# Reading activations backwards, weights in pairs and rows at other offsets in a two-block transformer kernel

## What is computed

```python
h = x
h = h + _hybrid_mixer(_rmsnorm(h, ...), ..., w_out)                 # 4 kinds of recurrent / linear attention heads
h = h + _memory_cross_attn(_rmsnorm(h, ...), mem_n, wq, wk, wv, wo) # attention on 256 memory rows
h = h + _conv_ffn(_rmsnorm(h, ...), w_up, conv_w, w_down)           # "ffn", 2 x 2816 columns up
x = _rmsnorm(h, final_norm_w)
for l in range(2):                                                  # the second block, DEPTH_2 = 2
    x, ctx = both through ffn_half_step(...)                        # "a1" for l = 0, "b1" for l = 1
    mixer: fourier_sgu_mixer for l = 0 ("ab_*"), attention with rope for l = 1 ("k2", "q2", "v2", "wo2")
    x (and ctx where it lives on) through ffn_half_step(...)        # "a2" for l = 0, "b2" for l = 1
return rms_norm(x, g_final_2)
```

## Time and profile before

| | |
|---|---|
| time, median of 2 runs | 2109.5 us (2108.54 and 2110.46) |
| profiled execution, span from the first to the last instruction | 2103.2 us |
| median less span | 6.3 us |
| TensorE busy | 2039.4 us, 97% |
| VectorE, ScalarE, GpSimd busy | 1172.1, 821.9, 225.2 us |

### The profile page before, as it was taken

One profiled execution on the slowest core, in us unless ns is written; L12 is line 12 of the kernel. 1 busy time (PEld: TensorE's weight loads), 2 busy tenths in 40 slices (PEclk: granted clock), 3 DMA queues, 4 the chain that ended last, 5 costly groups with the idle time before them and its releaser, 6 DMA issues.

```text
span 2103.2 us, 30887 instructions
## 1 busy us (share of the span) xinstructions
PE 2039.4 (97%) x13254; PEld 1787.7 (85%) x13254; DVE 1172.1 (56%) x1579; ACT 821.9 (39%) x1051; POOL 225.2 (11%) x185
## 2 busy tenths in 40 slices
PE   7988999999999999999999999999999999999998
PEld 6985998999888888888888888888888888878998
DVE  6778555767643654453555442235766744755454
ACT  6742455655532222243342222234222223455444
POOL 1000000403111001100101001110100111001111
PEclk9999999999999999999999999999999999999999
DMA  6425654454642543352344332234545533304553
GB/s 243 161 82 181 221 200 181 162 189 156 220 176 75 195 159 119 123 182 81 123 158 154 123 136 88 82 128 162 193 158 199 199 126 114 126 21 161 178 181 113
DMA packets 54136, 317.05 MB, mean 151 GB/s; under 512 B 6000, under 2 KB 12400, under 8 KB 23792
## 3 DMA queue, kind: packets, MB, share of 16 engines
q1 hardware_dynamic: 50848, 308.99, 41.4%
q10 hardware_dynamic: 3152, 6.10, 0.9%
HBM read 314.01 MB, written 1.05 MB: 150 GB/s over the span
## 4 chain that ended last, share of the span: by engine, by line
PE 86%; DVE 6%; ACT 4%; issue 3%; DMA 0%; SPq 0%; POOL 0%; DVEq 0%; ACTq 0%; POOLq 0%
PE psum L279 27%; PE psum L281 26%; PE psum L280 26%; ACT w_hi L255 2%; PE psum L1736 1%; PE psum L1334 1%; DVE w_lo L263 1%; PE psum L1317 1%; DVE xc L1525 0%; PE psum L1345 0%; DMA raw<-in_w_in_r 0%; PE psum L932 0%; DVE normed_lo L1916 0%; PE psum L933 0%; DVE small L1399 0%
## 5 line engine op out<-in xcount | busy, mean ns | idle before, releaser
L279 PE MATMUL psum<-normed_hi,w_hi 128*128 128x256 f32 (+1 forms) x2600 | 859.0, 330 | 18.5 <-DVE normed_lo L475 8.4
L280 PE MATMUL psum<-normed_lo,w_hi 128*128 128x256 f32 (+1 forms) x2600 | 848.3, 326 | 0.0
L281 PE MATMUL psum<-normed_hi,w_lo 128*128 128x256 f32 (+1 forms) x2600 | 848.0, 326 | 0.0
L263 DVE TENSOR_TENSOR w_lo<-raw,w_hi 128x2048 fp32r<-128x2048 f32 (+1 forms) x246 | 510.7, 2077 | 389.6 <-ACT w_hi L255 388.8
L279 PEld LDWEIGHTS psum<-normed_hi,w_hi 128*128 128x128 f32 x2600 | 492.2, 189 | 70.8 <-issue 21.9
L280 PEld LDWEIGHTS psum<-normed_lo,w_hi 128*128 128x128 f32 x2600 | 492.5, 189 | 43.3 <-issue 1.2
L281 PEld LDWEIGHTS psum<-normed_hi,w_lo 128*128 128x128 f32 x2600 | 492.4, 189 | 42.1
L255 ACT ACTIVATE w_hi<-raw 128x2048 fp32r<-128x2048 f32 (+1 forms) x246 | 421.7, 1714 | 161.7 <-PE psum L281 157.3
L279 PE MATMUL psum<-h_hi,w_hi 128*128 128x512 f32 (+1 forms) x913 | 310.7, 340 | 2.0 <-POOL h_lo L1681 1.7
L281 PE MATMUL psum<-h_hi,w_lo 128*128 128x512 f32 (+1 forms) x913 | 309.6, 339 | 0.0
L280 PE MATMUL psum<-h_lo,w_hi 128*128 128x512 f32 (+1 forms) x913 | 309.3, 339 | 0.0
(11 more groups left out here) (383 smaller groups left out, 1364.3 us busy)
## 6 DMA issues: line engine op xcount, KB each, us to landing
raw<-in_mod SPq DMA_DIRECT2D x72, 1024.0 KB, 4.8
raw<-in_a_up SPq DMA_DIRECT2D x42, 1024.0 KB, 4.8
raw<-in_b_up SPq DMA_DIRECT2D x42, 1024.0 KB, 4.8
raw<-in_ffn_up SPq DMA_DIRECT2D x22, 1024.0 KB, 4.8
raw<-in_a_down SPq DMA_DIRECT2D x32, 704.0 KB, 4.1
raw<-in_b_down SPq DMA_DIRECT2D x32, 704.0 KB, 4.1
raw<-in_ffn_down SPq DMA_DIRECT2D x16, 704.0 KB, 4.1
raw<-in_wo SPq DMA_DIRECT2D x8, 1024.0 KB, 4.7
```

The source lines that it names most:

```text
L263: dve.tensor_tensor(w_lo[:, slot, 0:size], raw[:, raw_slot(("main", g)), 0:size], w_hi[:, slot, 0:size].bitcast(F32), ALU.subtract).then_i ...
L279: pe.matmul(out, lh, rh, start=first, stop=False, skip_group_check=group)
L280: pe.matmul(out, lh, rl, start=False, stop=False, skip_group_check=group)
L281: return pe.matmul(out, ll, rh, start=False, stop=last, skip_group_check=group)
```

## The change

Three things are altered, stage by stage, by two tables of names.

- "backward": the moving activations are read from the last column to the first (`columns_of` gives a slice with step -1), and the output in PSUM is written from the last column to the first too (`made`), so each result lands where it was.
- "pairs": the split weights of a chunk lie interleaved, hi and lo of one weight side by side. ScalarE and VectorE write them, and LDWEIGHTS reads them, with a step of 8 bytes where it was 4. `w_hi` and `w_lo` are now one tensor, `w_parts`; in the other stages hi and lo are its two halves.
- rows: the hidden activations begin at column 40 (first half) and 24 (second half) in `ffn` and at column 12 in `b2`, where it was 8; the activations of both `up` jobs of `b1` begin at column 16, where it was 0.

The number and the order of the instructions on every engine stay as they were, and so do their shapes.

```diff
+WEIGHT_ORDER = {
+    "w_out": "backward", "wk": "pairs", "wq": "backward pairs",
+    "ffn_up0": "backward", "ffn_up1": "backward pairs",
+    "a1_up0": "backward", "a1_up1": "pairs", "a1_down0": "backward pairs", "a1_down1": "backward",
+    "a2_up0": "backward pairs", "a2_down0": "pairs",
+    "b1_up1": "backward", "q2": "pairs", "b2_up0": "backward", "b2_up1": "backward pairs",
+}
+HIDDEN_SHIFT = {"ffn": (40, 24), "b2": (12, 12)}
...
-        w_hi = sb("w_hi", [P, SLOTS, CHUNK], F32R)
-        w_lo = sb("w_lo", [P, SLOTS, CHUNK], F32R)
+        w_parts = sb("w_parts", [P, SLOTS, 2 * CHUNK], F32R)
+        w_hi, w_lo = w_parts[:, :, 0:CHUNK], w_parts[:, :, CHUNK:2 * CHUNK]
+        w_pair = w_parts[:, :, :].rearrange("p s (c two) -> p s c two", two=2)
...
+        def split_out(g, low):
+
+            slot, size = g % SLOTS, sizes[g]
+            if "pairs" in WEIGHT_ORDER.get(job_at[g], ""):
+                return w_pair[:, slot, 0:size, low]
+            return w_parts[:, slot, low * CHUNK:low * CHUNK + size]
+
+        def tile_of(s, i):
+
+            order = WEIGHT_ORDER.get(s.job.name, "")
+            cut = slice(i * P, (i + 1) * P)
+            if "pairs" in order:
+                return w_pair[:, s.slot, cut, 0], w_pair[:, s.slot, cut, 1]
+            return w_hi[:, s.slot, cut], w_lo[:, s.slot, cut]
+
+        def columns_of(s, cut):
+
+            if "backward" in WEIGHT_ORDER.get(s.job.name, ""):
+                return slice(cut.stop - 1, cut.start - 1 if cut.start else None, -1)
+            return cut
+
+        def moved(s, a, k, span):
+            return a[:, k, columns_of(s, span)]
+
+        def made(s, n, span):
+            return psum[:, s.bank + n, columns_of(s, span)]
...
-            act.activation(w_hi[:, slot, 0:size], raw[:, raw_slot(("main", g)), 0:size], ACT.Copy).then_inc(hi_ready, 1)
+            act.activation(split_out(g, 0), raw[:, raw_slot(("main", g)), 0:size], ACT.Copy).then_inc(hi_ready, 1)
...
-            dve.tensor_tensor(w_lo[:, slot, 0:size], raw[:, raw_slot(("main", g)), 0:size], w_hi[:, slot, 0:size].bitcast(F32),
+            dve.tensor_tensor(split_out(g, 1), raw[:, raw_slot(("main", g)), 0:size], split_out(g, 0).bitcast(F32),
...
-                            w = slice((n * k_tiles + k) * P, (n * k_tiles + k + 1) * P)
-                            mm = three_passes(pe, psum[:, s.bank + n, 0:span.stop - span.start],
-                                              (w_hi[:, s.slot, w], w_lo[:, s.slot, w]),
-                                              (act_hi[:, k, span], act_lo[:, k, span]), k == k_order[0], k == k_order[-1])
+                            w = n * k_tiles + k
+                            mm = three_passes(pe, made(s, n, slice(0, span.stop - span.start)),
+                                              tile_of(s, w),
+                                              (moved(s, act_hi, k, span), moved(s, act_lo, k, span)), k == k_order[0], k == k_order[-1])
...
-                self.hidden = slice(0, w) if w > T else slice(SHIFT, SHIFT + w)
+                self.hidden = [slice(at, at + w) for at in HIDDEN_SHIFT.get(name, (0, 0))]
...
+                self.hi, self.lo = (a[:, at:at + KT * 2 * T].rearrange("p (k t) -> p k t", k=KT) for a in (normed_hi, normed_lo))
...
-        n23, n24 = modulated_halves(3, "a2_down1"), modulated_halves(4, "b1_down1")
+        n23, n24 = modulated_halves(3, "a2_down1", at_column=16), modulated_halves(4, "b1_down1")
```

More of the change, by code:

```diff
@@ L245, in load @@
             sp.dma_start(raw[:, at % SLOTS, 0:size], src).then_inc(raw_landed[at % SLOTS], 16)
+        job_at = [job.name for job in jobs.values() for c in range(job.n)]
+        def split_out(g, low):
[17 more added lines that the diff above has]
+            return psum[:, s.bank + n, columns_of(s, span)]
         def split_hi(act, g):
@@ L313, in pe_begin @@
                 for n in range(2):
-                    w = slice((n * KT + k) * P, (n * KT + k + 1) * P)
-                    three_passes(pe, psum[:, s.bank + n, 0:span.stop - span.start], (w_hi[:, s.slot, w], w_lo[:, s.slot, w]),
-                                 (act_hi[:, k, span], act_lo[:, k, span]), k == 0, False)
+                    w = n * KT + k
+                    three_passes(pe, made(s, n, slice(0, span.stop - span.start)), tile_of(s, w),
+                                 (moved(s, act_hi, k, span), moved(s, act_lo, k, span)), k == 0, False)
         def pe_token_major(pe, job, act_hi, act_lo, span, after_tile=None, after_k=None):
@@ L347, in pe_tile_by_tile @@
                 for k in k_order:
-                    w = slice((n * k_tiles + k) * P, (n * k_tiles + k + 1) * P)
-                    mm = three_passes(pe, psum[:, s.bank + n, 0:T], (w_hi[:, s.slot, w], w_lo[:, s.slot, w]),
-                                      (act_hi[:, k, X], act_lo[:, k, X]), k == k_order[0], k == k_order[-1])
+                    w = n * k_tiles + k
+                    mm = three_passes(pe, made(s, n, X), tile_of(s, w),
+                                      (moved(s, act_hi, k, X), moved(s, act_lo, k, X)), k == k_order[0], k == k_order[-1])
                 if n == 0:
@@ L1575, in pe @@
                         before_down()
-                    pe_feature_major(pe, down, h_hi, h_lo, self.hidden, n_tiles=1, k_tiles=HALF, before_k=hidden_k,
+                    pe_feature_major(pe, down, h_hi, h_lo, self.hidden[half], n_tiles=1, k_tiles=HALF, before_k=hidden_k,
                                      in_halves={KT - 1: closing.pe_last} if half and closing is not None else None)
@@ L1603, in evac @@
                         act.wait_ge(evacuated, s.g + 1)
-                        out = h_hi[r, s.c:s.c + 1, self.hidden]
+                        out = h_hi[r, s.c:s.c + 1, self.hidden[half]]
                         act.activation(out, b[r, 1:2, 0:self.w], ACT.Copy).then_inc(ff_hi, 1)
@@ L1829, in pe_last @@
                                 self.pe_sums(pe, 0)
-                            w = slice((n * k_tiles + k) * P, (n * k_tiles + k + 1) * P)
-                            mm = three_passes(pe, psum[:, s.bank + h, n * T:(n + 1) * T], (w_hi[:, s.slot, w], w_lo[:, s.slot, w]),
-                                              (act_hi[:, k, t], act_lo[:, k, t]), at == 0, at == k_tiles - 1)
+                            w = n * k_tiles + k
+                            mm = three_passes(pe, made(s, h, slice(n * T, (n + 1) * T)), tile_of(s, w),
+                                              (moved(s, act_hi, k, t), moved(s, act_lo, k, t)), at == 0, at == k_tiles - 1)
                     if h == 0:
@@ L1845, in pe_first @@
                         for n in range(n_tiles):
-                            w = slice((n * k_tiles + k) * P, (n * k_tiles + k + 1) * P)
-                            mm = three_passes(pe, psum[:, s.bank + n, t], (w_hi[:, s.slot, w], w_lo[:, s.slot, w]),
-                                              (act_hi[:, k, t], act_lo[:, k, t]), k == 0, k == k_tiles - 1)
+                            w = n * k_tiles + k
+                            mm = three_passes(pe, made(s, n, t), tile_of(s, w),
+                                              (moved(s, act_hi, k, t), moved(s, act_lo, k, t)), k == 0, k == k_tiles - 1)
                 return mm
@@ L1881, in act_high_half @@
                     act.wait_ge(n_scaled, self.scaled_base + h * KT + k + 1)
[L1882 removed]
+                    act.activation(self.hi[:, k, t], nrm[:, k, t], ACT.Identity, bias=self.shift(k, h)).then_inc(n_hi, 1)
             def act_rest(self, act):
```

19 lines of the change are left out of this document (9 added, 10 removed).

## The result

The changed kernel takes 2134.8 us (2134.77 and 2134.88) where the kernel before takes 2109.5 us: ratio 1.0119, interval 1.0101 to 1.0138, or + 25.3 us. That is inside the range and within 2%, but it isn't the forecast of no change: all of the interval lies above 1.

A forecast was written before the change was run, and what follows sets the result against it. TensorE, busy 97% of the 2103.2 us span, bounds the kernel through its matmul paces. Zero for backward and pairs, - 0.3 us for ffn_down1, and 6.3 us from span to median gave 2109 us; range 2088 to 2175, the case's own 2095 to 2117.

The forecast's parts named there:

- I take zero for both: In the sum over touched TensorE stages: neither reading direction nor load step changes the pace, so backward and pairs add nothing.
- an effect of the size seen between two layouts, 3.3 ns: Upper bound for backward's 4,689 matmuls: the pace difference between aligned rows and rows shifted by 32 bytes at 256 columns.
- the prediction's own sign of being wrong: TensorE's pace within chunks: the forecast is wrong if several large stages move by over 5 ns.
- Pairs at 256 shifted columns: 888 matmuls of pairs with shifted rows: forecast zero; touched shifted stages losing 3.3 ns would add 5.4 us over 1,608 matmuls.
- 48 bytes: Rows at 12 columns in b2_down: 528 matmuls, between 0 and + 3.3 ns each, at most + 1.8 us.
- `ffn_down1`: Rows again 32 bytes behind a multiple of 64: 264 matmuls 1.1 ns faster if they take wk's rhythm, - 0.3 us.
- 64 bytes in `b1_up0`: Rows at 16 columns, a multiple of 64 bytes: claimed to cost nothing.
- The rival of pairs: Weight loads cost their reads twice: + 40 us (2149) if overhead doubles, + 153 us (2262) if load time doubles; chance 0.18.
- The rival of backward: Backward is a slow stream on TensorE: 9.0 ns per matmul makes 42 us, 14 ns + 66, half rate + 737; chance 0.12.
- The rule on the loads' step: SBUF lines are 16 bytes and two hits hide the access, so weight loads at an 8-byte step cost nothing.
- The streams out of each other's way: The change removes the per-matmul overhead of 13.3 or 10.0 ns on TensorE: wholly 72 us, giving 2037 us; chance 0.11.
- The splits: VectorE's stepped splits slow down and bound ffn_up1 (+ 9 us) and q2 (+ 2): + 11 us, 2120 us; chance 0.06.

The follow-up runs named there:

- u_rows: Changed kernel with only the moved rows kept, weights in one tensor as two halves, nothing backward or in pairs: 2111.7 us, ratio 1.0009.
- d_sides: Changed kernel with single causes per stage: only the read or only the output backward, weights some columns later, or pairs; some stages combined: 2133.2 us.
- s_rows1: Changed kernel with rows and weights at many different offsets, one combination per stage, all read forward and contiguous: 2124.8 us.
- s_apart: Kernel before with empty space between hi and lo activations, normed_lo 64 bytes and h_lo 128 bytes further on: 2130.6 us.
- n_narrow: Changed kernel with another table: in eight stages each weight load brings 64 columns instead of 128, half the outputs left out: 2117.7 us.
- best1: Kernel before with ffn_up0 and ffn_up1 backward, k2 and q2 rows at column 8, and h_lo pushed 128 bytes away: 2112.2 us, ratio 1.0016.

## Why the prediction was wrong

**The step that failed** is "I take zero for both" in the sum, with the bound under it, "an effect of the size seen between two layouts, 3.3 ns". The 3.3 ns is the difference between two layouts at 256 columns. At 512 columns showed one layout only, so there was no row for the effect there, and I put the same bound on it. The effect there is twice as large, and a loss: 233.3 less 226.7 is 6.7 ns (both rounded), for backward, for pairs and for both. 2,727 matmuls of 512 columns x 6.7 = + 18.2 us, and + 17.8 in the times of these stages. That is the prediction's own sign of being wrong: several large stages moved by over 5 ns. What the rows did show, that the offset moves the overhead and that one layout has several rhythms, should have widened the case's own range (2095 to 2117), not left zero as its middle. That 2134.8 lies in the stated range all the same is luck: the range reached so far because of the rivals, and none of them happened as priced.

**The other terms.** Pairs at 256 shifted columns: 888 matmuls, + 3.3 ns, + 2.9 us, the bound that I had written beside it. Pairs at 256 aligned columns (`q2`): nothing, as forecast. Backward at 256 aligned columns (`ffn_up0`): - 1.5 ns, which would be - 0.8 us, but - 0.3 us in the stage, as the distances across every second chunk edge grew from 0.31 to 0.39 us. At shifted ones `w_out` and `b2_up0` rose by 1 ns, but both have 117.7 to 117.9 in u_rows with no edit, so that isn't shown to be the price of backward. 48 bytes: + 0.8 us between 0 and 1.8. `ffn_down1`: + 0.5 us instead of - 0.3. 64 bytes in `b1_up0`: + 1.0 us instead of nothing; I had only the multiple of 64 in mind, and the untouched kernel has nothing at 512 columns that isn't at column 0.

**The rival of pairs** was right that pairs costs something, wrong in size and in its reason. 13.3 ns at aligned rows were 6.7 at 512 columns and 0 at 256, so the overhead doesn't go with the stretch that a load covers; no load took twice its time, as no stage came near 213 ns at 256 columns.

**The rival of backward** put the price on a slow stream, 9 ns or more. The stream costs 6.7 ns at 512 columns, - 1.5 at 256 aligned ones, and at shifted ones nothing that can be told from the 1 ns of untouched stages. The rule of the Trainium skill that stood beside it (Advanced Engine Details and Errata, PSUM Cachelines) doesn't bite on a descending output: written backward alone, `a1_up1` kept 226.8 ns.

**The rule on the loads' step.** The Trainium skill (Advanced Engine Details and Errata, SBUF Cachelines) asks for at least two hits on a line to hide the access. I read it as no cost for a step of 8 bytes. But TensorE's pace rose by 6.7 ns in `a1_up1` with nothing but pairs, and ScalarE's copy into the 8-byte step by 0.28 us, VectorE's by nothing. So in this case the step wasn't free for TensorE at 512 columns and for ScalarE, though two elements share a line; but reading backward, with contiguous columns, costs the same 6.7 ns, so the step isn't shown to be the reason as such.

**The streams out of each other's way** came true in `ffn_up0` alone, by 1.5 ns of 13.3. **The splits** I charged with 11 us or nothing; 1.2 us show in `ffn_up1`, by ScalarE's copy, which I had not looked at, and not by VectorE's.

**Two readings of the prediction** were off, and the forecast didn't rest on them: its 2,217 matmuls "of 512" columns hold 258 that run on 256, in the chunks made by halves, and from the earlier trace rows the room beside a load at 256 columns is 17 to 20 ns (117 to 120 less 100), not 10.

In the list of what would show it I named `b1_up1` for backward and `b1_up0` for 64 bytes; both did, at 233.3 and 228.8, though `b1_up1` has the 64 bytes as well. With backward alone (u_backward) it has 233.3 too.

**What stays open** is what the streams share. Shown: the cost of backward is in reading the moving operand, and the place of the load alone costs as well (d_sides); what counts of the places is each offset and not their difference alone (s_rows1), and the distance of the two moving tensors (s_apart); in `ffn_up1` the load's width counts too (n_narrow). Work of the other engines at the same moment isn't it: in `a1_up1` of the changed kernel the mean distance is 233.3 ns both while ScalarE, VectorE or GpSimd work and while all three rest (DMA not looked at). Against any one rule: a narrower load is slower in `wk` and at 512 columns, `b1_down0` and `b1_down1` of best1 differ by 4.4 ns in one layout, and `w_out`, `b2_up0` and `b2_up1` have two paces in one layout. That the two reads collide in SBUF is a guess which no run here isolates.
